# Moving the triangular inverses' transfers, the q/k spills and the k row sums by a few half tiles

## The reference

```python
lmat = jnp.where(strict, jnp.einsum('nbhid,nbhjd->nbhij', k_beta, kc) * decay, 0.0)
tmat = lax.linalg.triangular_solve(eye + lmat, eye, left_side=True, lower=True, unit_diagonal=True)
u = jnp.einsum('nbhij,nbhjd->nbhid', tmat, v_beta)
w = jnp.einsum('nbhij,nbhjd->nbhid', tmat, k_beta * jnp.exp(gc)[..., None])
...
q = apply_rope(rms_norm(qc.reshape(b, t, SA_HEADS, SA_HEAD_DIM), q_norm), cos_a, sin_a)
k = apply_rope(rms_norm(kc.reshape(b, t, SA_HEADS, SA_HEAD_DIM), k_norm), cos_a, sin_a)
```

## Time and profile before

| | us |
|---|---|
| median of 3 runs | 1989.96 (1988.85 to 1995.3) |
| the profiled execution: time | 1989.96 |
| its span in the trace | 1988.2 |
| PE busy | 1970.8 |
| DVE, ACT, POOL busy | 1042.3, 889.8, 858.5 |

### The profile page before, as it was taken

The page is one execution under the profiler, slowest core; times in us unless marked ns, Lnnn a source line. Parts: engine busy times, 40 slices in busy tenths (PEclk is TensorE's granted clock), DMA queues, the critical chain, the costliest instruction groups (busy, mean ns, idle before and its releaser), DMA issues.

```text
span 1988.2 us, 24453 instructions
## 1 busy us (share of the span) xinstructions
PE 1970.8 (99%) x9422; PEld 1562.9 (79%) x9422; DVE 1042.3 (52%) x1872; ACT 889.8 (45%) x1370; POOL 858.5 (43%) x646
## 2 busy tenths in 40 slices
PE   9999999999999999999999999999999999999999
PEld 6878878777788878787877788677777888888887
DVE  6657755655746568665365658476444346201210
ACT  5545543334345455633343355586455344312321
POOL 5445432443355444332334455455222456444443
PEclk9999999999999999999999999999999999999999
DMA  5334442423534235522424545322111332232232
GB/s 185 130 104 135 138 133 85 150 84 119 183 115 153 90 108 157 159 91 86 150 75 143 180 150 170 125 83 78 61 44 43 119 104 96 97 99 95 101 113 69
DMA packets 94851, 228.52 MB, mean 115 GB/s; under 512 B 29864, under 2 KB 32936, under 8 KB 93424
## 3 DMA queue, kind: packets, MB, share of 16 engines
q1 hardware_dynamic: 93264, 224.34, 34.0%
q10 hardware_dynamic: 1472, 2.62, 0.4%
HBM read 195.06 MB, written 24.64 MB: 111 GB/s over the span
## 4 chain that ended last, share of the span: by engine, by line
PE 85%; DVE 8%; ACT 3%; DMA 2%; SPq 1%; issue 1%; POOL 1%; ACTq 0%; DVEq 0%
PE bank L442 83%; PE bank L445 2%; DVE ER L376 1%; DVE kv L376 1%; SPq L371 1%; DMA gt<-gates 1%; DVE scs L401 1%; ACT lt L428 1%; POOL wl L376 1%; DMA kv<-blocks 1%; DVE tmp L386 1%; DVE m8s L398 0%; DVE nacc L376 0%; ACT L420 0%; DVE tmp L376 0%
## 5 line engine op out<-in xcount | busy, mean ns | idle before, releaser
L376 POOL TENSOR_TENSOR wl<-st,wh 128x512 fp32r<-128x512 f32 x606 | 812.7, 1364 | 1049.7 <-ACT wh L431 1049.7
L442 PE MATMUL bank<-hh,wh 128*128 128x512 f32 x1632 | 659.9, 404 | 4.9 <-DVE nacc L386 1.8
L442 PE MATMUL bank<-hh,wl 128*128 128x512 f32 x1632 | 637.3, 390 | 0.0
L442 PE MATMUL bank<-hl,wh 128*128 128x512 f32 x1632 | 636.7, 390 | 0.0
L431 ACT ACTIVATE wh<-st 128x1024 fp32r<-128x1024 f32 x303 | 318.7, 1052 | 237.9 <-PE bank L442 189.0
L442 PEld LDWEIGHTS bank<-hh,wh 128*128 128x128 f32 x1632 | 306.7, 188 | 96.8 <-issue 28.3
L442 PEld LDWEIGHTS bank<-hl,wh 128*128 128x128 f32 x1632 | 307.0, 188 | 67.5 <-issue 6.9
L442 PEld LDWEIGHTS bank<-hh,wl 128*128 128x128 f32 x1632 | 306.7, 188 | 65.4
L376 DVE TENSOR_TENSOR xt<-xt,bank 128x512 f32<-128x512 f32 x40 | 27.4, 687 | 235.6 <-PE bank L442 235.6
L428 ACT ACTIVATE tmp<-bank 128x512 f32<-128x512 f32 x70 | 41.7, 596 | 157.3 <-PE bank L442 150.7
L442 PE MATMUL bank<-fh,wh 128*128 128x512 f32 x256 | 99.6, 389 | 0.0
(11 more groups left out here) (337 smaller groups left out, 2932.9 us busy)
## 6 DMA issues: line engine op xcount, KB each, us to landing
st<-units SPq DMA_DIRECT2D x303, 512.0 KB, 3.5
gates<-tmp SPq DMA_DIRECT2D x48, 256.0 KB, 2.7
gt<-gates SPq DMA_DIRECT2D x48, 256.0 KB, 3.7
pad<-tmp SPq DMA_DIRECT2D x32, 128.0 KB, 2.7
qk<-tmp SPq DMA_DIRECT2D x16, 256.0 KB, 4.3
x_scratch<-xt SPq DMA_DIRECT2D x2, 2048.0 KB, 8.7
xt<-x_scratch SPq DMA_DIRECT2D x2, 2048.0 KB, 8.1
ph<-phi SPq DMA_DIRECT2D x8, 512.0 KB, 4.6
```

The source lines that it names most:

```text
L376: return NOTHING if self.e is None else self.e.tensor_tensor(out, a, b, op)
L442: return NOTHING if self.e is None else self.e.matmul(out, lhsT, rhs, start=start, stop=stop, skip_group_check=share)
```

## The change

In `delta` PE issues the spread of the k sums one step later, and DVE waits for it one step later; ACT's transpose of the inverses and its two DMAs stand one step earlier; on SP the write of the inverses stands three steps later, directly before the reads. In `proj` SP's spill of a q or k row stands four steps earlier. No arithmetic, shape or buffer changes.

```diff
@@ tensor_program, delta
             spread(aa4[0], "dn", l, 0)
             yield
+            yield
             spread(aa4[1], "dn", l, 1)
-            yield
             yield
@@ scalar_program, delta
-            yield from idle(INVERSE - BACK + 6)
+            yield from idle(INVERSE - BACK + 5)
             ac.wait_ge(*at("inv", l, 31))
...
-            yield from idle(BACK - 6)
+            yield from idle(BACK - 5)
@@ vector_program, delta
                 yield
-                if f == 0:
-                    yield
+                yield
                 dv.wait_ge(*at("dn_up", l, f))
...
-            yield
             yield
@@ sync_program, proj, row
-                yield from idle(7)
+                yield
+                yield
+                yield
                 sp.wait_ge(*at("qk_o", l, c))
@@ sync_program, delta
-            yield from idle(INVERSE - BACK + 2)
+            yield from idle(INVERSE - BACK + 5)
+            sp.wait_ge(*at("x_zero", l, False))
+            sp.wait_ge(*at("x_zero", l, True))
             sp.wait_ge(*at("inv", l, 31))
...
-            yield from idle(3)
-            sp.wait_ge(*at("x_zero", l, False))
-            sp.wait_ge(*at("x_zero", l, True))
             sp.wait_ge(*at("inverses", l, 1))
             sp.wait_ge(*at("inverses_t", l, 1))
```

## The result

The changed kernel took 2005.41 us, median of 4 runs (2004.59 to 2006.94), against 1990.9 us for the kernel before in the same comparison (1988.85 to 1995.3, 4 runs): the ratio is 1.0067 with a 95% interval of 1.0055 to 1.008. The forecast was 1998.5, +8.5; measured are +14.5 between the medians and +0.67%, about 13.3 us, by the ratio. The direction was right and the size was not: the time lies 1.4 us above the range of 1994 to 2004.

A forecast was written before the change was run, and what follows sets the result against it. PE, busy 1970.8 of 1988.2 us, was taken as the bound. Later first use of X, +4.0 in layer 0 (first term inside the second) and +4.5 in layer 1, gave 1989.96 + 8.5 = 1998.5; range 1994 to 2004.

The forecast's parts named there:

- The k spread, 0 us: Spread twelve matmuls later ends by 137.3; DVE takes its result only at 137.97, so it costs 0 us.
- The first term: ACT's earlier transpose waits for DVE, delaying row 5's squares to 239.42; PE's sum of nr stands 3.0 us.
- The relief of DVE: POOL's work withheld with ACT's cast: two DVE operations shrink from 1.26 to about 0.29, inversion done 1.94 us earlier.
- The second term: SP's write of the inverses leaves at 242.7, reads follow; layer 0 first uses X at 256.0 instead of 251.99, +4.0.
- The rule weighed in the prediction: Trainium skill's DMA fit, fixed 2.0 us plus bytes over 436 GB/s: half the write would land in 2.3 us.
- Layer 1, +4.5: Layer 1 repeats layer 0 579.3 us later, so X is first used at 835.3 instead of 830.76.
- The spills, 0 us: SP stands about 18 us at row 3's early spill, but loads behind it still land in time: 0 us.
- The first one behind the wait can only be cast at 237: The unit load behind SP's wait at row 3's spill, issued from 230.3, lands before ACT can cast it: 0 us.
- Not slower: Rival: ACT's wait is free, XT arrives in time and both PE waits, 1.3 us, go: 1988.6; chance 0.04.
- only the squares count: Rival: write and reads land fast, PE's own 254.1 decides; +2.1 and +2.6, 1994.7; chance 0.16.
- No relief, slow reads: Rival: DVE still finishes at 236.67 and reads keep their old pace; +7.2 and +7.7, 2004.9; chance 0.14.

The follow-up runs named there:

- e1: Kernel before with only the k spread (PE's issue and DVE's wait) moved one step later; 1994.78 us, ratio 1.0013.
- after: The changed kernel, all four moves made on the kernel before; 2005.41 us, ratio 1.0067.
- e9: Changed kernel with the k spread put back at its old place; 2002.8 us, ratio 1.0047.
- e4: Kernel before with only the write of the inverses moved directly ahead of the reads; 1987.15 us, ratio 0.9979.
- e11: Changed kernel with useless matmuls filling PE's waits ahead of row 5's sum and the first use of X; 2004.2 us, ratio 1.006.
- e5: Kernel before with only the spills of q and k rows moved four tiles earlier; 1994.6 us, ratio 1.0016.
- e6: Kernel before with the spills and the write of the inverses moved; 2004.05 us, ratio 1.0068.
- e13: Kernel before with the write and the spills moved, except row 4's spill, left at its old place; 1998.54 us, ratio 1.0034.
- e7: Changed kernel with the spills of the rows put back at their old place; 2000.78 us, ratio 1.0046.
- e12: Changed kernel with the write of the inverses put back at its old place; 2000.85 us, ratio 1.0042.
- e2: Kernel before with only ACT's transpose of the inverses and its DMAs moved one step earlier; 1998.11 us, ratio 1.0023.
- e3: Kernel before with ACT's transpose and DMAs one step earlier, plus ten useless matmuls ahead of row 5's sum; 1992.4 us, ratio 1.0001.
- e10: Kernel before with the k spread moved and DVE's k products put ahead of its index-key operations; 1990.0 us, ratio 0.9991.
- e14: Kernel before with write and k spread moved, DVE's k products ahead of its index-key operations; 1986.49 us, ratio 0.9969.

## Why the prediction was right or wrong

**The k spread, 0 us: the step that failed first.** It measured 2.6 us alone (e1) and 2.6 to 3.9 in after (e9). With the spread at its old place the other three moves take 2002.8 us, inside the range. The prediction asked only if the spread's result was there when DVE took it at 137.97. It was; but DVE took it later, since POOL's work slid beside DVE's. The same shift moves all that comes later: row 3's spill leaves at 232.11 instead of 229.80.

**The first term, 3.0 us: right.** The wait on `nr` is 2.64 and 2.65. The relief of DVE came: its two operations of 128 columns take 0.29 each in after,

```profile
232.68 0.29 DVE L376 TENSOR_TENSOR ER<-kv 128x128 f32<-128x128 f32 x1
233.00 0.29 DVE L376 TENSOR_TENSOR kv<-kv,ER 128x128 f32<-128x128 f32 x1
```

against 1.26. But it is given back: POOL's withheld low halves start at 240.49,

```profile
240.49 5.88 POOL L376 TENSOR_TENSOR wl<-st,wh 128x512 fp32r<-128x512 f32 x4 [9.68 <-ACT wh L431]
```

beside row 4's last two operations, 1.73 and 1.65 instead of 0.69. These stand ahead of row 4's spill, and so of the write.

**The second term in layer 0: right mechanism, too small.** X is used at 261.46, where 256.0 was forecast. The 5.46 us are: 2.31 of the k spread; 1.58 by which the write is later still (246.59 against 242.7 plus 2.31), which DVE's two stretched operations, 2.0 together, more than cover; 0.86 of landing (6.76 from first issue to first read, against 5.9); 0.71 of the reads (8.11 against 7.4, the last landing in 4.31 instead of 2.76). This tells where the time lies, not that the parts are independent: without the k spread (e9) X is used at 256.26, so that 5.20 of the 5.46 go with it, not 2.31. The rule weighed in the prediction would have had a half of the write landed in 2.3 us; the halves' median in after is 5.7, and in e4, with the least beside them, 4.3. The Trainium skill, "DMA: Bandwidth & Descriptors", "Specifications", says that transfers under 512 bytes do not reach line rate. The write's pieces are 64 bytes. ACT's write of the transposed inverses moves the same 128 KB in pieces of 2 KB; its halves land in 3.3 us in e4 and 4.0 in after, where those of SP's write take 4.3 and 5.7, so the traces agree in kind, though queue and moment differ too.

**The lower clock: missing.** Between X and the end of layer 0's stage after loses another 2.3 us (DVE's `X<-vf` at 328.23 against 316.49, 11.74 late, where X was 9.47 late). A sum made of waits alone can't hold it, and it does not come with every wait. What it costs in the end stays open, as e11 shows.

**Layer 1, +4.5: 6.4 measured** (913.52 against 895.39 is 18.13, less 11.74): `kf` 2.3, `nr` 2.65, and about 1.5 left for the clock, which is 0.83 in 830 to 835. XT's wait is 0.34, less than the 0.41 before: here PE's own lateness and the write's are the same.

**The spills, 0 us: wrong.** Alone they cost 3.2 (e5). With the write in its new place they make 17.7, from -4.2 (e4) to +13.5 (e6); e13 lays 11.0 of it on the spills of the other rows and 6.7 on row 4's. "The first one behind the wait can only be cast at 237" held with ACT's move and not without: in e5 and e13 ACT waits 2.05 and 2.55 us for it. The sum did count row 4's spill ahead of the write, in the second term; it was not seen that the moved write is a gain, -4.2, where nothing else is moved (e4). In company it is not: beside k spread and ACT's move the gain is gone (e7), and from e12 to after, with the spills there too, the moved write costs 4.9.

**The rivals.** "Not slower" and "only the squares count" fell with the write at 246.59. "No relief, slow reads", 2004.9, has nearly the time but not the reasons: the relief is there and the reads are slow by 0.7.

## What to carry to other kernels

In an in-order queue, a transfer that others wait for should have nothing ahead of it that waits long for a different engine: the same move of a write gained 4.2 us alone, and together with spills that cost 3.2 alone it lost 13.5. The effects of such moves do not add, so each pair has to be measured. A change that makes a piece of work shorter or later slides another engine's work under someone else's operations; look for the operations that it then runs beside, and not only for who waits for the moved result. And a wait of the engine that bounds the kernel can cost more than its length where that engine is TensorE: look at the granted clock behind it.

## What the runs showed of the hardware

- The granted clock falls behind or within some short stalls of PE and not with others, and the stall's length does not tell which: in the window of 5 us at its end or behind it the clock was 0.65 for a wait of 1.43 us (e9, 715 to 720), 0.70 for 1.82 (e1, 140 to 145), 0.66 for 2.75 (e2) and 0.50 for 3.52 (after), but 1.00 for 2.34 (after, layer 1's `kf`), 2.95 (e2, layer 1) and 2.97 (e9, layer 1's X). At the lower level a matmul of 128x512 takes 0.63 us for 0.39, and they start 0.43 apart for 0.23. With matmuls of no use in the gap it stayed at 1.00 (e3, e11).
- A good part of the scatter between runs of one kernel goes with this clock. Of 76 runs of the kernel before, beside the experiments, the 32 with a mean clock of 1.000 took 1990.7 us on the mean, and the 9 with 0.997 took 1995.5.
- DVE operations with two SBUF inputs of 128x512 take 0.69 us, and often 1.5 to 1.8 while POOL forms a low half (not always: one of 0.68 in e10 starts at 137.60, inside POOL's row of 136.38 to 139.41). The Trainium skill, "Advanced Engine Details and Errata", "GPSIMD Details", says that the two share an interface for such operations; most of the rows agree.
- The write of the inverses keeps SP's queue busy for 1.6 to 2.1 us in the kernel before, e1 to e4, e10 and e14, and for 3.1 to 3.8 us in after, e5 to e9 and e11 to e13, for the same two DMAs. What makes the second half issue later stays open.
